# One hybrid decoder layer: K's evacuation on two engines, norm vectors loaded earlier, FFN transposes in one place per group

## The reference, cut to what matters

```python
h = rmsnorm(x, pre_mix_norm)
rq, rk, rv, rg, mq, mk, mv = split(h @ w_in)            # 1024 x 3072
ret = silu(rg) * head_rmsnorm(retention(rotary(rq), rotary(rk), rv))
moba = softmax(mq @ mk.T / 8 + bias, causal) @ mv       # one block of 256 keys
x = x + rmsnorm(concat(ret, moba) @ w_out, post_mix_norm)
h = rmsnorm(x, pre_ffn_norm)
f = (silu(h @ w_gate) * (h @ w_up)) @ w_down            # 1024 x 2816, twice; 2816 x 1024
x = x + rmsnorm(f, post_ffn_norm)
```

## Time and profile before

| | |
|---|---|
| median of 3 runs | 316.71 us (316.2 to 316.86) |
| profiled execution: its own time | 318.91 us |
| profiled execution: span from first to last instruction | 317.1 us |
| busy, PE | 305.3 us, 96% of the span |
| busy, PE weight loads | 248.8 us, 78% |
| busy, DVE / ACT / POOL | 182.7 / 153.3 / 27.6 us |
| chain that ended last, by engine | PE 85%, DVE 7%, ACT 3%, DMA 2%, POOL 2%, issue 1% |
| bytes read from memory | 57.10 MB |

### The profile page before, as it was taken

How to read it: one execution, slowest core, us unless ns; L and a number is a source line. 1 busy time by engine, 2 the same in 40 slices (tenths; PEclk the granted TensorE clock), 3 DMA queues, 4 the chain that set the end, 5 groups by cost and what they waited for, 6 DMA issues and landing times.

```text
span 317.1 us, 4124 instructions
## 1 busy us (share of the span) xinstructions
PE 305.3 (96%) x1432; PEld 248.8 (78%) x1432; DVE 182.7 (58%) x255; ACT 153.3 (48%) x254; POOL 27.6 (9%) x31
## 2 busy tenths in 40 slices
PE   7999987999999999999999999999999999999992
PEld 3788866888888888768888888888888888888881
DVE  2858265697467487899555555544444454551426
ACT  4889626446608174676444444444433333340322
POOL 4021056000002000540000000000000000000001
PEclk9999999999999999999999999999999999999999
DMA  6999974314541543169965555555566565400003
GB/s 216 398 407 373 413 308 134 134 66 153 180 144 57 198 156 111 66 231 317 367 203 179 179 190 180 168 184 191 198 198 198 198 196 183 149 0 0 0 2 132
DMA packets 17517, 58.35 MB, mean 184 GB/s; under 512 B 1997, under 2 KB 2517, under 8 KB 17504
## 3 DMA queue, kind: packets, MB, share of 16 engines
q1 hardware_dynamic: 17136, 57.06, 51.6%
q0 software_dynamic: 368, 1.11, 1.0%
HBM read 57.10 MB, written 1.06 MB: 183 GB/s over the span
## 4 chain that ended last, share of the span: by engine, by line
PE 85%; DVE 7%; ACT 3%; DMA 2%; POOL 2%; issue 1%; SPq 0%; DVEq 0%
PE bank L951 25%; PE bank L953 24%; PE bank L952 24%; PE bank L961 4%; DVE w_lo L681 2%; DMA raw<-in_w_in 2%; PE bank L978 1%; POOL xs L437 1%; PE bank L982 1%; PE bank L986 1%; ACT w_hi L451 1%; DVE d_lo L876 1%; ACT kz L518 1%; PE bank L1049 1%; DVE res L942 1%
## 5 line engine op out<-in xcount | busy, mean ns | idle before, releaser
L951 PE MATMUL bank<-w_hi,a_hi 128*128 128x512 f32 x256 | 101.9, 398 | 0.0
L953 PE MATMUL bank<-w_hi,a_lo 128*128 128x512 f32 x256 | 100.1, 391 | 0.0
L952 PE MATMUL bank<-w_lo,a_hi 128*128 128x512 f32 x256 | 99.6, 389 | 0.0
L617 ACT ACTIVATE sil<-bank,rstd 128x256 f32<-128x256 f32 x22 | 10.4, 473 | 96.1 <-PE bank L953 93.7
L953 PEld LDWEIGHTS bank<-w_hi,a_lo 128*128 128x128 f32 x256 | 48.0, 188 | 10.6
L952 PEld LDWEIGHTS bank<-w_lo,a_hi 128*128 128x128 f32 x256 | 48.2, 188 | 9.8
L951 PEld LDWEIGHTS bank<-w_hi,a_hi 128*128 128x128 f32 x256 | 48.1, 188 | 9.4
L869 DVE TENSOR_TENSOR w_lo<-raw,w_hi 128x1024 fp32r<-128x1024 f32 x40 | 49.6, 1276 | 6.7 <-ACT w_hi L602 6.7
L681 DVE TENSOR_TENSOR w_lo<-raw,w_hi 128x1024 fp32r<-128x1024 f32 x32 | 42.2, 1345 | 19.4 <-ACT w_hi L451 19.4
L884 DVE SCALAR_TENSOR_TENSOR hid<-bank,rstd,sil 128x256 f32<-128x256 f32 x22 | 10.7, 485 | 73.9 <-ACT sil L617 73.9
L602 ACT ACTIVATE w_hi<-raw 128x1024 fp32r<-128x1024 f32 x40 | 40.5, 1057 | 0.5 <-DMA raw<-in_w_gu 0.5
(11 more groups left out here) (119 smaller groups left out, 307.5 us busy)
## 6 DMA issues: line engine op xcount, KB each, us to landing
raw<-in_w_gu SPq DMA_DIRECT2D x44, 512.0 KB, 4.3
raw<-in_w_dn SPq DMA_DIRECT2D x22, 512.0 KB, 4.6
raw<-in_w_in SPq DMA_DIRECT2D x20, 512.0 KB, 8.5
raw<-in_w_out SPq DMA_DIRECT2D x8, 512.0 KB, 3.2
raw<-in_w_in SPq DMA_DIRECT2D x8, 256.0 KB, 5.8
xs<-in_x SPq DMA_DIRECT2D x2, 512.0 KB, 8.6
bias<-bias_row POOLq DMA_DIRECT2D x1, 1024.0 KB, 10.2
out<-res SPq DMA_DIRECT2D x4, 256.0 KB, 2.0
```

The lines of the kernel that those rows point to most:

```text
L617: act.activation(sil[:, t, :], pg[:, t, 0:FG], ACT.Silu, scale=rstd[:, X1_, t:t + 1]).then_inc(sil_ready[t], 1)
L951: pe.matmul(acc, hi, wh, start=first, stop=False)
L952: pe.matmul(acc, hi, wl, start=False, stop=False)
L953: return pe.matmul(acc, lo, wh, start=False, stop=last)
```

## The change

Four things change.

1. The half of the transposed K on partitions 64 to 127 is copied to `kz` by DVE (two new instructions, semaphore `kT_odd`), the other half by ACT as before (two instructions instead of four).
2. `gp` and `gm` are issued behind units 10 and 11. On ACT the evacuations of Q, K and V (`rows_out`) stand ahead of the high part of their step, not behind it.
3. In the FFN both token blocks of a group's `hid` are transposed in one place, between `down(g - 1, 0)` and `down(g - 1, 1)`. Those of group 0 stand inside `gate_up(1, 1)`, behind its second unit.
4. The group with index 1 (the second) has its gate and up in banks 4 and 5 and doesn't wait for `hidden(0, t)`; group 0's transposes go to banks 0 and 1.

```diff
+        def pg(g):
+            return bank45 if isinstance(g, int) and g == 1 else bank01
+        def pt(g):
+            return bank01 if isinstance(g, int) and g == 0 else bank45
...
-                if n == 16:
+                if n == 10:
                     sp.dma_start(gp[:, :], g_pre_ffn.broadcast_to([P, D])).then_inc(gp_loaded, 16)
-                if n == 18:
+                if n == 11:
                     sp.dma_start(gm[:, :], g_post_mix.broadcast_to([P, D])).then_inc(gm_loaded, 16)
...
                         act.wait_ge(k_turned, t + 1)
-                        for odd in range(2):
-                            rows = slice(64 * odd, 64 * odd + 64)
-                            act.activation(kz[rows, odd:MH:2, t * P:(t + 1) * P],
-                                           wk[rows, t, :].rearrange("p (b i) -> p b i", i=P), ACT.Copy
-                                           ).then_inc(kT_ready, 1)
+                        act.activation(kz[0:64, 0:MH:2, t * P:(t + 1) * P],
+                                       wk[0:64, t, :].rearrange("p (b i) -> p b i", i=P), ACT.Copy
+                                       ).then_inc(kT_ready, 1)
+                if u == UPG:
+                    act.wait_ge(nq_ready, 1)
+                    wait_factor(act, X_, NT - 1)
+                    rows_out(qn, 0, lambda t: nq[:, t:t + 1], q_nat)
+                if u == 2 * UPG:
+                    rows_out(kn, 1, r_x, k_nat)
+                if u == 3 * UPG:
+                    rows_out(v, 2, r_x, v_nat)
                 hi_in(u + LEAD)
...
             def group(g, g0, more=True):      # ACT; DVE alike with h_lo_part, lo_gu, hidden
+                if g0 > 1:
+                    h_hi_part(g - 1, 1)
                 if more:
                     for s in range(GU - 1):
                         hi_gu(g + 1, s, g0 + 1)
                 silu(g, 0)
-                h_hi_part(g - 1, 1)
+                if g0 == 1:
+                    for t in range(NT):
+                        h_hi_part(0, t)
...
             for u in range(N_IN):             # DVE
+                if u == K_T + 1:
+                    for t in range(NT):
+                        dve.wait_ge(k_turned, t + 1)
+                        dve.tensor_copy(kz[64:P, 1:MH:2, t * P:(t + 1) * P],
+                                        wk[64:P, t, :].rearrange("p (b i) -> p b i", i=P)
+                                        ).then_inc(kT_odd, 1)
...
                     if h == 0:
                         pe.wait_ge(kz_zeroed, 2)
-                        pe.wait_ge(kT_ready, 2 * NT)
+                        pe.wait_ge(kT_ready, NT)
+                        pe.wait_ge(kT_odd, NT)
...
             def gate_up(g, t, g0, hook=None):
-                if not (isinstance(g, int) and g == 0):
+                if not (isinstance(g, int) and g <= 1):
                     pe.wait_ge(hid_ready[t], g)
...
+            def first_hidden(s):
+                if s == 1:
+                    for t in range(NT):
+                        turn_hidden(0, t)
             def group(g, g0):                 # PE
-                gate_up(g, 0, g0)
-                turn_hidden(g - 1, 1)
+                for t in range(NT):
+                    gate_up(g, t, g0, hook=first_hidden if g0 == 1 and t == 1 else None)
                 down(g - 1, 0, g0 - 1)
-                gate_up(g, 1, g0)
-                turn_hidden(g, 0)
+                for t in range(NT):
+                    turn_hidden(g, t)
                 down(g - 1, 1, g0 - 1)
```

More of the change, by code:

```diff
@@ L161, in hybrid_layer @@
         ph = bank45
-        pg = bank01
-        pt = bank45
+        def pg(g):
+            return bank45 if isinstance(g, int) and g == 1 else bank01
+        def pt(g):
+            return bank01 if isinstance(g, int) and g == 0 else bank45
         pf = [bank67, bank23]
@@ L211, in hybrid_layer @@
         kT_ready = sem("kT_ready")
+        kT_odd = sem("kT_odd")
         kz_zeroed = sem("kz_zeroed")
@@ L529, in _ @@
                         squares(X_, u, c, xs[:, u, c * CW:(c + 1) * CW])
[L530 to L537, removed]
                 if u == RQK_T + 1:
@@ L616, in silu @@
                     act.wait_ge(hid_ready[t], g)
-                act.activation(sil[:, t, :], pg[:, t, 0:FG], ACT.Silu, scale=rstd[:, X1_, t:t + 1]
+                act.activation(sil[:, t, :], pg(g)[:, t, 0:FG], ACT.Silu, scale=rstd[:, X1_, t:t + 1]
                                ).then_inc(sil_ready[t], 1)
@@ L623, in h_hi_part @@
                     wait_down(act, g - 1, t)
-                act.activation(h_hi[:, t, :, :], pt[:, t, 0:FG].rearrange("p (b i) -> p b i", i=P),
+                act.activation(h_hi[:, t, :, :], pt(g)[:, t, 0:FG].rearrange("p (b i) -> p b i", i=P),
                                ACT.Copy).then_inc(hhi_ready[t], 1)
             def group(g, g0, more=True):
+                if g0 > 1:
+                    h_hi_part(g - 1, 1)
                 if more:
@@ L653, in _ @@
             silu(0, 1)
-            h_hi_part(0, 0)
             hi_dn(0, 1, 0)
@@ L883, in hidden @@
                     dve.wait_ge(h_turned[t], g)
-                dve.scalar_tensor_tensor(out=hid[:, t, :], in0=pg[:, t, FG:2 * FG],
+                dve.scalar_tensor_tensor(out=hid[:, t, :], in0=pg(g)[:, t, FG:2 * FG],
                                          scalar=rstd[:, X1_, t:t + 1], in1=sil[:, t, :],
@@ L889, in h_lo_part @@
                 dve.wait_ge(hhi_ready[t], g + 1)
-                dve.tensor_tensor(h_lo[:, t, :, :], pt[:, t, 0:FG].rearrange("p (b i) -> p b i", i=P),
+                dve.tensor_tensor(h_lo[:, t, :, :], pt(g)[:, t, 0:FG].rearrange("p (b i) -> p b i", i=P),
                                   h_hi[:, t, :, :].bitcast(F32), ALU.subtract).then_inc(hlo_ready[t], 1)
             def group(g, g0, more=True):
+                if g0 > 1:
+                    h_lo_part(g - 1, 1)
                 if more:
@@ L897, in group @@
                 hidden(g, 0)
-                h_lo_part(g - 1, 1)
+                if g0 == 1:
+                    for t in range(NT):
+                        h_lo_part(0, t)
                 if more:
@@ L918, in _ @@
             hidden(0, 1)
-            h_lo_part(0, 0)
             lo_dn(0, 1, 0)
@@ L1154, in gate_up @@
                             pe.wait_ge(alo_ready, 2 * t + k // 4 + 1)
-                        ins = product(pg[:, t, :], a_hi[:, k, tile(t)], a_lo[:, k, tile(t)],
+                        ins = product(pg(g)[:, t, :], a_hi[:, k, tile(t)], a_lo[:, k, tile(t)],
                                       w_hi[:, a0 % RING, i * CW:(i + 1) * CW],
@@ L1169, in turn_hidden @@
                     pe.wait_ge(hlo_ready[t], g)
-                turn(pt[:, t, :], hid[:, t, :], DN, h_turned[t])
+                turn(pt(g)[:, t, :], hid[:, t, :], DN, h_turned[t])
             def down(g, t, g0, last=False):
@@ L1206, in _ @@
             gate_up(0, 1, 0)
-            turn_hidden(0, 0)
             group(1, 1)
@@ L1212, in _ @@
             group(NF - 1, NF - 1)
-            turn_hidden(NF - 1, 1)
             down(NF - 1, 0, NF - 1, last=True)
```

## The result

The changed kernel takes **319.74 us**, the median of nine runs (318.19 to 320.88), beside 316.72 us before (nine runs, 316.12 to 319.22). The ratio is 1.0082, with a 95% interval of 1.0053 to 1.0111: slower by 0.8%, 3 us. Forecast were 317.0 us and no change, in a range that ended at 318.9.

The account below looks back on a forecast made before the run. PE was taken as the bound, busy 305.3 of 317.1 us. Scores +0.05, the FFN's start +0.2 and the rest of the FFN 0 made +0.25 us on the median 316.71: 317.0 us, no measurable change, range 314.1 to 318.9.

Parts of the forecast that it names:

- Place 1, the collision: Attention scores: DVE low parts and POOL multiplications exclude each other, K's copies end at 42.6, head 0 loses 3.3 us.
- DVE's sum: Before K's copies: 3 x 2.40 us of POOL plus 3 x 1.1 of low parts, 10.5 us from 30.85 to 41.35.
- the signs that it named: Scores: 3 us wait at head 0, POOL between 30 and 39, low parts over 2; FFN's start: 2 us of waits.
- Place 1, the sum "3.3 - 3.25 = +0.05": Scores: new loss at head 0 against both old waits vanishing, +0.05 us net, between -0.6 and +1.5.
- the -3.25: Scores of heads 2 and 3: old losses of 1.31 + 1.94 us, both claimed to vanish with the change.
- Rival A: Scores: old waits smaller in timed runs than in the profile, head 2's 1.31 us absent; 318.3 us, chance 0.28.
- Rival B: Scores: low parts 12 to 14 not held up, head 0 loses 0.6 instead of 3.3; 314.2 us, chance 0.20.
- C: FFN's start: DVE not late, `hidden(1, 1)` ready at 149.5, 1.2 us come off; 315.8 us, chance 0.10.
- Place 2, the FFN's start: Old waits gone, new losses of 0.4, 0.4 and 1.2 us on DVE's list: +0.2 us, between -0.6 and +0.8.
- The rest of the FFN: Later FFN groups: one place of transposes instead of two saves nothing, no load runs late; 0 us.
- 0.11 each however many stand together: FFN transposes: eight take 0.87 us, four 0.44, so putting them in one place saves nothing.
- K on two engines "buys nothing": Scores: splitting K's copies leaves ACT 1.2 us instead of 2.44, no gain claimed since ACT isn't late.

Follow-up runs that it names:

- experiment 1: The changed kernel with twelve extra matmuls, results thrown away, on PE in front of its wait for K's copies: 318.11 us, ratio 1.0036 to before.
- experiment 4: The changed kernel with the FFN as before, K on two engines and early norm vectors kept: 320.03 us, ratio 1.0069.
- experiment 5: The kernel before, unchanged, run again for a second profile: 316.95 us, ratio 1.0013 to its twin.
- Experiment 7: The kernel before with the FFN part of the change alone: 316.48 us, ratio 0.9993.
- experiment 3: The changed kernel with the loads of `gp` and `gm` back behind units 16 and 18: 315.91 us, ratio 0.9945.
- experiment 9: The changed kernel with each of POOL's three multiplications cut into quarters: 317.68 us, ratio 1.0018 to before.

## Why the prediction was wrong

**Place 1, the collision: right in size, and in part by luck.** POOL from 29.46 to 38.47 (forecast: from 30), DVE's copies done at 42.02 (42.6), head 0's loss 3.0 us (3.3), heads 2 and 3 without a wait. The way there was another. The working let DVE and POOL take turns without a pause from 30.85 on and put all three multiplications, 3 x 2.40 us, in front of K. In the trace DVE stands idle for 1.54 and 2.56 us in that stretch, waiting for high parts. On the chain to K's copies stand the landing of unit 13 (35.19), its high part and then one multiplication, which ends at 38.47 and holds low part 13 up from 36.30 on. The prediction had unit 13 near 35 itself and left it out of DVE's sum; what it put in too much and too little nearly cancels. Of the signs that it named nearly all came (the first low part beside POOL took 1.81 us, not over 2), and the time was outside the range all the same.

**Place 1, the sum "3.3 - 3.25 = +0.05": this step failed, in two ways.** First, it priced the idle time at its length. A wait of 3.0 us at one place and two of 1.3 and 1.9 us are not the same: behind the one PE worked at 1.2 GHz, which cost 2.9 us more in this execution (experiment 1 takes them away with the wait in place), 1.6 us in the one of experiment 4 and as much by the medians. I read "granted clock was full in all slices" and didn't ask whether it would stay so. Second, the -3.25 belongs to the profiled execution and not to the median: usually it is -1.3 (experiment 5).

With both repaired it is 316.7 + 1.35 = 318.1 us with the clock left alone (experiment 1 measured 318.1), 319.7 with 1.6 us lost to it and 321.0 with 2.9. The runs go from 318.2 to 320.9.

**Rival A: true,** and it was given 0.28. Its 318.3 us is where the three runs lie whose clock hardly fell. That is in part luck: it took off 1.31 us where the profiles differ by 1.9, and the FFN was 0.6 us better than either had it. I held against it that three runs within 0.7 us showed no jumps; with 15 of 69 runs in the slower group, three in a row without one are what is seen about every other time. **Rival B** (low parts not held up) didn't come about; **C** (`hidden(1, 1)` in time) didn't either, 0.89 us idle.

**Place 2, the FFN's start: right** in its sum, +0.24 for +0.2. Its three waits came, 0.4, 0.1 and 1.1 us for 0.4, 0.4 and 1.2; that the sum fits all the same is due to small delays that I haven't followed. **The rest of the FFN** was put at 0 and was -0.6 us: the term "0.11 each however many stand together" left out that a second place of transposes costs some 0.06 us a group besides the transposes themselves. Experiment 7's times are too coarse to show it; the profiles show it in each group.

**K on two engines "buys nothing": open.** With the early loads it does harm. Between the kernel before and the one with the loads back (experiment 3), where it stands with two other parts (ACT's new order and the FFN), 1.1 us are gained. Which of the three gives them was not taken apart.

What stays open: what decides, from run to run, whether and for how long the clock falls behind a wait of 1.7 to 3 us. And the 0.17 us left over at the scores.

## What to carry to other kernels

Work that keeps another engine out of its memory isn't made harmless by moving it; list what stands behind the instruction that it will hold up, and cut it into pieces short enough that nobody waits (here quarters, 0.5% faster, though POOL itself took a third longer for the first two). Price an idle stretch of TensorE of some 3 us with the slow matmuls that follow it, here up to as much again, and don't strike it off against two shorter ones. And where the profiled execution lies 2 us above the median, look for a race of 0.1 us in it before its waits go into a sum.

## What the runs showed of the hardware

- The granted clock fell to 0.50 within an idle stretch of 3.2 us between matmul starts (38.93 to 42.17) and came back only 6 us after work had begun again. In experiment 4, with a stretch of the same length, it fell only when work began again and was back less than 4 us later (1.00 from 46.0). Stretches of 1.54, 2.17 and, in experiment 9, 2.1 us left it at 1.00.
- The same kernel runs at a mean clock of 0.987 in one execution and 0.997 in another, with 2.7 us between their times.
- A GpSimd multiplication and a VectorE subtraction in SBUF take turns by whole instructions: with POOL 0.31 us ahead a low part took 3.17 us, with DVE 0.09 us ahead 1.23 us. With quarters (0.95 us each on average, with the time that POOL stood still) low parts took 1.2 to 1.7 us.
- Copies out of PSUM don't take part in this: 1.30 us for K's two beside the quarters (39.22) as without POOL (39.20).
